# The ends of two mixers: norm weights and squares taken at the eviction, row sums accumulated in the residual sum

## Chip, core and metric

One core of one Trainium2 chip runs one program. The metric is device time in microseconds from start to end of an execution; the kernel before takes 2954.93 us, the median of three executions (2954.92 to 2955.82).

## What is computed

Two transformer-like blocks run one after the other over 1024 positions of width 1024, all in float32. Only the places where a mixer ends matter here.

```python
# first block, after its mixer (state space + Fourier + window attention)
y = concatenate([y_ssm, y_fft, y_att]) @ w_out
x = x + gt_m * rms_norm(y, g_post_mix)
h = rms_norm(x, g_pre_ffn) * (1.0 + sc_f) + sh_f
up = dwconv3(h @ w_up, conv_w, conv_b)
...
# second block, after its mixer (sparse attention + gated MLP)
m = mixer(x) ; x = layernorm(ALPHA * x + m, ln2_g, ln2_b)
x = layernorm(ALPHA * x + 0.5 * swiglu(x, ffn2_w1, ffn2_w3, ffn2_w2), ln3_g, ln3_b)
```

rms_norm divides by the root of the mean square of a row; layernorm takes off the mean of a row and divides by the root of its variance. Both then multiply by a weight per column, and layernorm adds a bias per column.

## The kernel before

The 1024 positions are eight row tiles (n = 0 to 7) of 128 positions; the width is eight column tiles (k = 0 to 7). Each product of float32 is three products of upper and lower parts (fp32r), so each operand is first split: ScalarE writes the upper part (a cast), VectorE the lower part (source less upper part). TensorE, VectorE, ScalarE and SyncE each have an order of instructions written out by hand, and semaphores between them (`wait_ge`, `then_inc`).

**The mixer's last product** (`down_tensor`, `down_products` L1083). It has two halves of four row tiles. Each half accumulates over eight steps and leaves the four rows in PSUM, two banks for a row (`y_banks(n)`). The first half is evicted while the second is multiplied, and its norm and residual sum are made there (`end_piece_scalar`, `end_piece_vector`). The change leaves that as it is. What it touches is what comes behind the second half, when the rows 4 to 7 finish in the order 6, 7, 4, 5 (`last_rows`).

**What comes behind it** (`end_tensor_up`). The next stage is the product with the up weights. TensorE first transposes rows 0 to 3 (the left half of the new operand, columns k = 0 to 7, L2540) into the banks that the evicted rows leave, then makes the first "classic" product with each column (L1983) as soon as its lower part is there (`x_lo_made`); after that rows 4 to 7 in the same way (the right half). It can start to transpose rows 4 to 7 when these are complete: in the first mixer when they are scaled (`row_scaled`, L2187), in the second when the final row operation is done (`row_ready`, L2285).

**First mixer's end** (`end_scalar`, `end_vector` with e = 0). ScalarE evicts rows 6 and 4 by copies (L2213), VectorE rows 7 and 5 (L2247). VectorE scales and shifts each transposed column into `split_tmp` (L2378), ScalarE casts it (L2356), VectorE makes the lower part (L2372). Between odd columns ScalarE squares a row of y and sums it (`square_row` L2120). Then follow, with nothing of the split left: factors (`norm_factors`: mean square L2069, root on ScalarE L2058, five small steps in `inverse_root` L3731 to L3739), for each row `add_branch` (two multiplications by factor and norm weight L2180, one addition L2183), its square on ScalarE, factors again, and `scale_rows` (L2187). The norm weight is in `row_a`.

**Second mixer's end** (the same functions with e = 3). VectorE adds the residual while it evicts (L2253), makes the lower parts straight from PSUM (L2372), and between columns 3 to 6 the moments of a row (`row_moments`, bn_stats L2191 and bn_aggr L2193). `last_factors` then centres and weights the rows (L2282), takes the roots and applies factor and bias (L2285).

**Behind both**: `upper_second` on ScalarE and `lower_second` on VectorE split the right half's columns, with four sums of parts ahead (`first_sum`, L1637). SyncE loads the weights (L1494) and stores the finished rows (`end_store` L2103).

Of the kernel before, what the change touches and what calls it, by code (L numbers as in the profile page):

```python
# [61 lines left out]
def body(ctx, nc, a, out):  # L62
# [764 lines left out]
    before = {"units": 0, "evac": 0, "ups": 0, "act": 0}  # L827

    class Down:


        def __init__(self, d, e, src, w, split_ahead, rest_ahead, first=None):
# [9 lines left out]
            before["evac"] += 4 if e < 2 else 2  # L842
# [148 lines left out]
    res_in, sq_done, var_ready, std_ready, row_ready = (sem(n) for n in ("res_in", "sq_done", "var_ready", "std_ready", "row_ready"))  # L991
    row_scaled, cols_turned, cols_hi, cols_ready = (sem(n) for n in ("row_scaled", "cols_turned", "cols_hi", "cols_ready"))
# [94 lines left out]
    def down_tensor(pe, st):  # L1087
        t = nc.tensor

        def step(half, k, kk, j, slot):  # L1090
# [3 lines left out]
            for n in rows_left:  # L1094
                if first and half:
                    pe.wait_ge((evac_act, evac_dve)[n % 2], st.evacs + n // 2 + 1)
# [1025 lines left out]
    def end_piece_scalar(act, st, i):  # L2122
        e = st.e
        if e == 0:
            if i == 0:
                act.wait_ge(evac_act, st.evacs + 2)
                act.wait_ge(evac_dve, st.evacs + 2)
# [21 lines left out]
    def end_piece_vector(dve, v, steps, st, i):  # L2149
# [12 lines left out]
        elif 0 <= i < 4:  # L2162
            dve.wait_ge(res_in, 16 * (NT * e + i + 1))
            if i == 0:
                dve.wait_ge(evac_act, st.evacs + 2)
                dve.wait_ge(evac_dve, st.evacs + 2)
# [37 lines left out]

    def end_scalar(act, st, up):

        s, e = nc.scalar, st.e
        for u in range(2):
            up_begin_scalar(act, up, u)
        if e == 0:  # L2210
            for n in (HN + 2, HN):
                st.wait_row(act, 1, n - HN)
                s.copy(y_row(n), y_banks(n)).then_inc(evac_act, 1)  # L2213
        upper_first(act, up)
        take_root(act, cols_of(1))
        if e == 0:
            for n in rows_of(1):
                square_row(act, n, True)
            take_root(act, cols_of(1))
        cast_op(act, up, 1, 0)  # L2220
        upper_second(act, up)

# [16 lines left out]

    def end_vector(dve, v, steps, st, up):  # L2240
# [3 lines left out]
        if e == 0:  # L2244
            for n in (HN + 3, HN + 1):
                st.wait_row(dve, 1, n - HN)
                v.tensor_copy(y_row(n), y_banks(n)).then_inc(evac_dve, 1)  # L2247
        else:
            dve.wait_ge(res_in, 16 * NT * (e + 1))
            for n in st.last_rows[1]:  # L2250
                n = HN + n
                st.wait_row(dve, 1, n - HN)
                v.scalar_tensor_tensor(res(n), y_banks(n), Y_SCALE[e], res(n), ALU.mult, ALU.add).then_inc(y_used, 1)  # L2253
        def moments_between(k):
            if 3 <= k < 3 + HN:
                row_moments(v, steps, HN + k - 3)

        if e:
            dve.wait_ge(y_used, HN)
        lower_first(dve, v, up, moments_between)  # L2260
        if e == 0:
            dve.wait_ge(evac_act, st.evacs + 4)
            dve.wait_ge(evac_dve, st.evacs + 4)
            dve.wait_ge(sq_done, 3 * HN)
            norm_factors(dve, v, steps, stat_a[:, cols_of(1)], cols_of(1))
            for n in rows_of(1):
                add_branch(dve, v, steps, n)
            dve.wait_ge(sq_done, 2 * NT)
            norm_factors(dve, v, steps, stat_c[:, cols_of(1)], cols_of(1))
            dve.wait_ge(xt_turned, up.turned(0, KD - 1))  # L2270
            scale_rows(v, 1)
        else:
            last_factors(dve, v, steps, e)
# [75 lines left out]
    def upper_first(act, up):  # L2349

        s, e = nc.scalar, up.e
        for k in range(KD):
            upper = x_columns(0, k)[0]
            if e == 0:
                act.wait_ge(xt_tmp, TMP_0 + k + 1)
                s.copy(upper, split_tmp[k % 2][:]).then_inc(x_hi_made, 1)  # L2356
            else:
                act.wait_ge(xt_turned, up.turned(0, k))
                s.copy(upper, turn_bank(k)).then_inc(x_hi_made, 1)
            if e == 0 and k % 2:  # L2360
                if k == 1:
                    act.wait_ge(evac_act, 4)
                    act.wait_ge(evac_dve, 4)
                square_row(act, HN + k // 2, False)

    def lower_first(dve, v, up, between=None):

        def rest(k):
            upper, lower = x_columns(0, k)
            dve.wait_ge(x_hi_made, up.turned(0, k))  # L2370
            src = split_tmp[k % 2][:] if up.e == 0 else turn_bank(k)
            v.tensor_tensor(lower, src, upper, ALU.subtract).then_inc(x_lo_made, 1)  # L2372
        if up.e == 0:
            for k in range(KD):
                dve.wait_ge(xt_turned, up.turned(0, k))
                if k >= 2:
                    dve.wait_ge(x_lo_made, up.turned(0, k - 2))
                v.tensor_scalar(split_tmp[k % 2][:], turn_bank(k), mod_cols[:, 3, k:k + 1], mod_cols[:, 2, k:k + 1],  # L2378
                                ALU.mult, ALU.add).then_inc(xt_tmp, 1)
                if k:  # L2380
                    rest(k - 1)
# [1925 lines left out]
```

## Time and profile before

| | |
|---|---|
| median of three executions | 2954.93 us |
| the profiled execution | 2953.73 us |
| its span | 2951.9 us |
| busy: TensorE, VectorE, ScalarE | 96%, 72%, 45% |
| mean granted TensorE clock | 0.981 of full |
| end of the first mixer | about 484 to 520 us |
| end of the second mixer | about 2271 to 2302 us |

The profile is one execution. TensorE's busy time overlaps with its loads of weights, so 96% means that it hardly ever has nothing under way, not that it runs at its peak. The full clock is 2.4 GHz; a granted clock of 0.5 is 1.2 GHz. All points in time are from the span's start.

### The profile page before, as it was taken

The page shows a single profiled execution, that of the slowest core. Times are in us where ns is not written, and L with a number is a line of the kernel's source. Part 1 is how long each engine was busy: PE and PEld are TensorE (multiplying, and loading weights), DVE is VectorE, ACT ScalarE, POOL GpSimd, SP SyncE. Part 2 cuts the span into 40 slices and gives each one's busy share as a digit, 9 for nine tenths or more (in the row PEclk, how much of TensorE's full clock was granted, in tenths as well). Part 3 has the DMA queues.
Part 4 walks back from the last instruction along what each step waited for, and adds up shares of the span by engine and source line. Part 5 has one row for each costly group of instructions (what it writes and reads, how often), then busy time and mean ns, then how long its engine had stood idle before and what let it go on. Part 6 is the DMA issues. An engine that isn't in the chain of part 4 may idle for free.

```text
span 2951.9 us, 37423 instructions
## 1 busy us (share of the span) xinstructions
PE 2820.3 (96%) x13573; PEld 2259.0 (77%) x13573; DVE 2119.2 (72%) x3861; ACT 1321.5 (45%) x2324; POOL 197.9 (7%) x250
## 2 busy tenths in 40 slices
PE   7998997999999999999999999999999899999997
PEld 4885676788888888788888887786677688888886
DVE  7888638888988567766666667798737866666568
ACT  3124745544444454433333453577743433333443
POOL 2050000000000000000000000223610000000000
PEclk9989999999999999999999999999999999999999
DMA  6542043244445884344447753211033344545864
GB/s 232 159 142 38 9 136 121 82 164 163 152 156 189 275 264 138 110 155 152 160 164 270 257 188 108 54 44 34 1 108 114 110 153 162 164 163 190 300 195 144
DMA packets 345413, 436.83 MB, mean 148 GB/s; under 512 B 29685, under 2 KB 191517, under 8 KB 345054
## 3 DMA queue, kind: packets, MB, share of 16 engines
q1 hardware_dynamic: 342274, 428.46, 44.5%
q10 hardware_dynamic: 2956, 5.99, 0.6%
q8 instruction: 108, 1.77, 0.2%
q14 instruction: 75, 0.61, 0.1%
HBM read 317.59 MB, written 116.50 MB: 147 GB/s over the span
## 4 chain that ended last, share of the span: by engine, by line
PE 79%; DVE 12%; ACT 4%; DMA 2%; issue 2%; POOL 1%; ACTq 0%; DVEq 0%; SPq 0%
PE psum L1992 37%; PE psum L1443 21%; PE psum L1083 5%; PE psum L2872 4%; PE psum L1983 3%; PE psum L4218 1%; DVE count_junk L3403 1%; PE psum L3075 1%; DMA ada_piece<-in_w_ada 1%; PE psum L3088 1%; PE psum L3062 1%; DMA x_rows<-in_x 1%; DVE x_t L1689 1%; ACT probs L499 1%; DVE ada_acc L3938 1%
## 5 line engine op out<-in xcount | busy, mean ns | idle before, releaser
L1443 PE MATMUL psum<-far_op,far_op 128*128 128x512 f32 x2772 | 629.6, 389 | 0.1
L1443 PEld LDWEIGHTS psum<-far_op,far_op 128*128 128x128 f32 x2772 | 520.2, 188 | 108.3 <-issue 0.5
L1992 PE MATMUL psum<-x_b,w_near 128*128 128x512 f32 x1440 | 346.0, 389 | 0.8 <-DVE w_near L1615 0.8
L1992 PE MATMUL psum<-x_t,w_near 128*128 128x512 f32 x1440 | 337.1, 389 | 2.3 <-ACT psum L1729 2.3
L1992 PE MATMUL psum<-x_t,w_far 128*128 128x512 f32 x1440 | 336.3, 389 | 0.0
L1992 PEld LDWEIGHTS psum<-x_t,w_near 128*128 128x128 f32 x1440 | 270.1, 188 | 59.5 <-ACT psum L1729 3.6
L1992 PEld LDWEIGHTS psum<-x_b,w_near 128*128 128x128 f32 x1440 | 270.3, 188 | 57.3 <-issue 1.2
L1992 PEld LDWEIGHTS psum<-x_t,w_far 128*128 128x128 f32 x1440 | 270.3, 188 | 56.4 <-ACT u_keep L1741 0.3
L1214 DVE TENSOR_TENSOR far_op<-far_a,far_op 128x512 fp32r<-128x512 f32 x231 | 159.7, 691 | 176.1 <-ACT far_op L1207 174.9
L1207 ACT CAST far_op<-far_a 128x512 fp32r<-128x512 f32 x231 | 143.9, 623 | 316.3 <-PE psum L1443 308.1
L1992 PE MATMUL psum<-x_b,w_far 128*128 128x512 f32 x720 | 177.9, 397 | 9.1 <-DVE val_row L1861 9.1
L1992 PEld LDWEIGHTS psum<-x_b,w_far 128*128 128x128 f32 x720 | 138.3, 193 | 39.4 <-DVE val_row L1861 10.3
L1615 DVE TENSOR_TENSOR w_far<-w_sum,w_far 128x512 fp32r<-128x512 f32 x120 | 82.3, 686 | 111.5 <-ACT w_far L1609 111.5
L1216 DVE TENSOR_TENSOR far_op<-far_b,far_op 128x512 fp32r<-128x512 f32 x231 | 159.1, 689 | 0.0
L3538 POOL TENSOR_TENSOR split_lo<-raw,split_hi 128x256 fp32r<-128x256 f32 (+1 forms) x60 | 44.8, 781 | 1642.2 <-ACT split_hi L2888 1642.2
L1208 ACT CAST far_op<-far_b 128x512 fp32r<-128x512 f32 x231 | 142.1, 615 | 0.0
L1615 DVE TENSOR_TENSOR w_near<-w_sum,w_near 128x512 fp32r<-128x512 f32 x120 | 80.9, 687 | 73.4 <-ACT w_near L1609 73.4
L1609 ACT CAST w_far<-w_sum 128x512 fp32r<-128x512 f32 x120 | 73.9, 616 | 114.3 <-PE psum L1992 114.3
L1609 ACT CAST w_near<-raw 128x512 fp32r<-128x512 f32 (+1 forms) x129 | 82.8, 642 | 70.5 <-PE psum L1992 59.1
L1615 DVE TENSOR_TENSOR w_far<-raw,w_far 128x512 fp32r<-128x512 f32 (+1 forms) x66 | 47.2, 715 | 84.8 <-ACT w_far L1609 84.8
L1060 DVE TENSOR_TENSOR src_lo<-yc_t,src_hi 128x512 fp32r<-128x512 f32 x31 | 21.4, 692 | 119.6 <-ACT w_out_hi L1053 119.5
L1983 PE MATMUL psum<-x_b,w_near 128*128 128x512 f32 x360 | 91.9, 406 | 7.3 <-DVE x_b L2372 6.4
(522 smaller groups left out, 4834.7 us busy)
## 6 DMA issues: line engine op xcount, KB each, us to landing
far_a<-row_ops SPq DMA_DIRECT2D x231, 256.0 KB, 2.9
row_ops<-hidden SPq DMA_DIRECT2D x99, 512.0 KB, 5.6
raw<-in_ffn_w SPq DMA_DIRECT2D x88, 512.0 KB, 4.3
col_sums<-hidden SPq DMA_DIRECT2D x66, 512.0 KB, 5.6
far_b<-col_sums SPq DMA_DIRECT2D x132, 256.0 KB, 3.5
raw<-in_w_up SPq DMA_DIRECT2D x44, 512.0 KB, 3.9
hidden<-in_ffn_w SPq DMA_DIRECT2D x44, 512.0 KB, 5.0
far_b<-in_ffn_w SPq DMA_DIRECT2D x66, 256.0 KB, 3.3
```

The costliest lines, as they stand in the source:

```text
L1083: ins = t.matmul(bank(2 * n + c), l[:, P * n:P * (n + 1)], r[:, HALF * c:HALF * (c + 1)], start=(first and m == 0), stop=(last and m == 2))
L1207: s.copy(far_a_hi[slot][:], far_a[late][t % FB][:]).then_inc(f_hi, 1)
L1208: s.copy(far_b_hi[slot][:], far_b[late][t % FB][:]).then_inc(f_hi, 1)
L1214: v.tensor_tensor(far_a_lo[slot][:], far_a[late][t % FB][:], far_a_hi[slot][:], ALU.subtract).then_inc(f_lo, 1)
L1216: v.tensor_tensor(far_b_lo[slot][:], far_b[late][t % FB][:], far_b_hi[slot][:], ALU.subtract).then_inc(f_lo, 1)
L1443: ins = t.matmul(bank(b + n), l[slot][:, rows], r[slot][:], start=(fresh and i == 0 and m == 0), stop=(i == FH - 1 and m == 2), skip_group ...
L1609: nc.scalar.copy(op_parts(p, i)[0], op_source(p, i)).then_inc(op_hi, 1)
L1615: nc.vector.tensor_tensor(lower, op_source(p, i), upper, ALU.subtract).then_inc(op_lo, 1)
L1983: ins = t.matmul(bank(b), at[:, l, cols], r, start=(first and m == 0), stop=(last and m == 2))
L1992: ins = t.matmul(bank(b), at[:, l, cols], x[:, k, r], start=(start and k == 0 and m == 0), stop=(k == 3 and m == 2), skip_group_check=not ...
L2872: ins = t.matmul(bank(2 * slot + half)[0:m], l[:, P * k:P * k + m], r[:, k, HALF * half:HALF * (half + 1)], start=(k == 0 and i == 0), sto ...
L3538: ins = g.tensor_tensor(tile_of(w_rest, m)[:, k:k + 2], tile_of(raw[slot], m)[:, k:k + 2], tile_of(w_top, m)[:, k:k + 2], ALU.subtract)
```

## The change

In the first mixer's end (`mix_end_scalar`, `mix_end_vector`) VectorE evicts all four rows and multiplies them by the norm weight as it does; ScalarE squares the rows straight from PSUM. A row's banks are read by one engine at a time, by turns. ScalarE scales, shifts and casts the left half's columns; VectorE makes the lower parts and, between them, the residual sum of a row with one instruction. The squares of the finished rows stand between the columns on ScalarE. Two rows are scaled on VectorE, two on ScalarE. One operand cast goes behind the second column of the right half.

In the second mixer's end the residual sum also accumulates the sum of its row. From it comes the negative mean; ScalarE squares the row with that as its bias and accumulates, between its casts; VectorE centres and weights a row behind it, between its lower parts. bn_stats and bn_aggr are gone there. The first half's waits on evictions now count each engine's by itself (`st.evacs`).

```diff
+    SQUARED, GAINED_FIRST = (2, 0, 3, 1), (2, 3, 1)
+    def mix_end_scalar(act, st, up):
+        def square_banks(n):
+            st.wait_row(act, 1, n)
+            act.wait_ge(sq_done, 2 * HN + SQUARED.index(n))
+            if n in GAINED_FIRST:
+                act.wait_ge(evac_dve, st.evacs[1] + 2 + left.index(n) + 1)
+            s.activation(sq_junk[:], y_banks(HN + n), ACT.Square, accum_out=stat_a[:, HN + n:HN + n + 1]).then_inc(sq_done, 1)
+        up_begin_scalar(act, up, 0)
+        up_begin_scalar(act, up, 1)
+        for n in SQUARED[:3]:
+            square_banks(n)
+        for k in range(KD):
+            act.wait_ge(xt_turned, up.turned(0, k))
+            if k >= 2:
+                act.wait_ge(x_lo_made, up.turned(0, k - 2))
+            s.activation(split_tmp[k % 2][:], turn_bank(k), ACT.Identity, scale=mod_cols[:, 3, k:k + 1],
+                         bias=mod_cols[:, 2, k:k + 1]).then_inc(xt_tmp, 1)
+            act.wait_ge(xt_tmp, TMP_0 + k + 1)
+            s.copy(x_columns(0, k)[0], split_tmp[k % 2][:]).then_inc(x_hi_made, 1)
+            if k == 0:
+                square_banks(SQUARED[3])
+                take_root(act, cols_of(1))
+            elif 3 <= k < 3 + HN:
+                square_row(act, HN + k - 3, True)
+                if k == 2 + HN:
+                    take_root(act, cols_of(1))
+        act.wait_ge(rstd_ready, 1)
+        act.wait_ge(xt_turned, up.turned(0, KD - 1))
+        for n in rows_of(1)[2:]:
+            s.mul(scaled_row(n), res(n), rstd(n)).then_inc(row_scaled, 1)
+        upper_second(act, up, lambda: cast_op(act, up, 1, 0))
+    def spread_rows(act, k):
+        at = {3: (0, 1), 4: (2,), 5: (3,)}.get(k, ())
+        if k == 3:
+            act.wait_ge(mean_ready, 1)
+        for i in at:
+            n = HN + i
+            if i:
+                act.wait_ge(spread_ready, i)
+            nc.scalar.activation(sq_junk[:], res(n), ACT.Square, bias=stat_c[:, n:n + 1],
+                                 accum_out=stat_a[:, n:n + 1]).then_inc(spread_ready, 1)
+        if k == KD - 1:
+            take_root(act, cols_of(1))
+    def mix_end_vector(dve, v, steps, st, up):
+        def gained(n):
+            st.wait_row(dve, 1, n)
+            if n not in GAINED_FIRST:
+                dve.wait_ge(sq_done, 2 * HN + SQUARED.index(n) + 1)
+            v.tensor_tensor(y_row(HN + n), y_banks(HN + n), wide(row_a), ALU.mult).then_inc(evac_dve, 1)
...
+        up_begin_vector(dve, up, 0)
+        for n in left[:2]:
+            gained(n)
+        up_begin_vector(dve, up, 1)
+        for n in left[2:]:
+            gained(n)
+        rest(0)
+        dve.wait_ge(sq_done, 3 * HN)
+        begin_factors(stat_a[:, cols_of(1)])
+        end_root(dve, v, steps, cols_of(1), False)
+        dve.wait_ge(evac_dve, st.evacs[1] + 2 + HN)
+        for k in range(1, 1 + HN):
+            rest(k)
+            n = HN + k - 1
+            dve.wait_ge(res_in, 16 * (n + 1))
+            v.scalar_tensor_tensor(res(n), y_row(n), rstd(n), res(n), ALU.mult, ALU.add).then_inc(row_ready, 1)
+        for k in range(1 + HN, KD - 1):
+            rest(k)
+        dve.wait_ge(sq_done, 2 * NT)
+        begin_factors(stat_c[:, cols_of(1)])
+        end_root(dve, v, steps, cols_of(1), False)
+        dve.sem_inc(rstd_ready, 1)
+        rest(KD - 1)
+        dve.wait_ge(xt_turned, up.turned(0, KD - 1))
+        for n in rows_of(1)[:2]:
+            v.tensor_scalar(scaled_row(n), res(n), rstd(n), None, ALU.mult).then_inc(row_scaled, 1)
+        lower_second(dve, v, up)
     def end_vector(dve, v, steps, st, up):
...
+            v.scalar_tensor_tensor(res(n), y_banks(n), Y_SCALE[e], res(n), ALU.mult, ALU.add,
+                                   accum_out=stat_c[:, NT + n:NT + n + 1]).then_inc(y_used, 1)
+        dve.wait_ge(y_used, HN)
+        steps.add(v.tensor_scalar(stat_c[:, cols_of(1)], stat_c[:, NT + HN:2 * NT], -1.0 / D, None, ALU.mult))
+        steps.settle()
+        dve.sem_inc(mean_ready, 1)
+        def centre_between(k):
             if 3 <= k < 3 + HN:
-                row_moments(v, steps, HN + k - 3)
+                n = HN + k - 3
+                dve.wait_ge(spread_ready, k - 2)
+                steps.add(v.scalar_tensor_tensor(res(n), res(n), stat_c[:, n:n + 1], wide(row_a), ALU.add, ALU.mult))
+            if k == 2 + HN:
+                steps.add(v.tensor_scalar(stat_a[:, NT + HN:2 * NT], stat_a[:, cols_of(1)], 1.0 / D, LN_EPS / ALPHA ** 2, ALU.mult, ALU.add))
+                steps.settle()
+                dve.sem_inc(var_ready, 1)
+        lower_first(dve, v, up, centre_between)
+        end_root(dve, v, steps, cols_of(1), False)
+        for n in rows_of(1):
+            v.scalar_tensor_tensor(res(n), res(n), rstd(n), wide(row_b), ALU.mult, ALU.add).then_inc(row_ready, 1)
...
     def end_tensor_up(pe, st, up):
             if e == 0:
-                pe.wait_ge((evac_act, evac_dve)[n % 2], st.evacs + (3 if n >= HN - 2 else 4))
+                at = st.last_rows[1].index(n)
+                pe.wait_ge(sq_done, 2 * HN + SQUARED.index(n) + 1)
+                pe.wait_ge(evac_dve, st.evacs[1] + 2 + at + 1)
```

`rest(k)` in `mix_end_vector` is the lower part of column k (L2372), and `begin_factors` the mean square (L2069).

## Rows read from the trace of the kernel before

**Rows 1.** The page's first part: busy us and share of each engine.
```profile
PE 2820.3 (96%) x13573; PEld 2259.0 (77%) x13573; DVE 2119.2 (72%) x3861; ACT 1321.5 (45%) x2324; POOL 197.9 (7%) x250
```
**Rows 2.** Waits of TensorE, 470 to 620: total us, times, longest.
```profile
PE psum L2540 <- DVE hidden L2187: 14.7, 1, 14.7
```
**Rows 3.** Waits of TensorE, 2260 to 2420.
```profile
PE psum L2540 <- DVE hidden L2285: 8.3, 1, 8.3
```
**Rows 4.** Windows, first mixer's end: busy by engine, granted clock, DMA share, GB/s.
```profile
488.00:501.00 13.00, 13.00 (x64) 10.48 (x64) 11.37 (x21) 7.74 (x15) 0.00 (x0) 1.00 0.09 23
501.00:515.70 14.70, 0.05 (x1) 0.00 (x0) 12.85 (x22) 5.74 (x10) 0.00 (x0) 0.63 0.38 143
515.70:519.80 4.10, 3.33 (x17) 3.09 (x17) 3.12 (x6) 2.85 (x5) 0.00 (x0) 0.65 0.00 0
...
545.00:580.00 35.00, 29.85 (x122) 23.37 (x121) 33.63 (x48) 17.10 (x28) 0.00 (x0) 0.95 0.35 113
```
**Rows 5.** Windows, second mixer's end.
```profile
2271.00:2277.00 6.00, 2.39 (x18) 1.71 (x16) 5.96 (x7) 2.14 (x4) 0.00 (x0) 1.00 1.04 321
...
2290.00:2298.40 8.40, 0.15 (x2) 0.02 (x1) 8.23 (x13) 0.00 (x0) 0.00 (x0) 0.71 0.30 111
2298.40:2302.00 3.60, 3.60 (x17) 3.60 (x18) 3.60 (x7) 1.80 (x4) 0.00 (x0) 0.50 1.03 354
```
**Rows 6.** In order of time, first mixer: start, us, instruction [idle before <-releaser].
```profile
482.14 1.92 ACT L2213 COPY hidden<-psum 128x1024 f32<-128x1024 f32 x2
...
483.49 2.35 DVE L2247 COPY hidden<-psum 128x1024 f32<-128x1024 f32 x2
...
487.98 1.66 PE L1983 MATMUL psum<-x_b,w_near 128*128 128x512 f32 x6 [2.00 <-DVE x_b L2372]
...
502.48 1.06 ACT L2120 ACTIVATE sq_junk<-hidden 128x1024 f32<-128x1024 f32 x1 [3.75 <-DVE hidden L2183]
503.45 0.19 ACT L2120 ACTIVATION_READ_ACCUMULATOR sq_junk<-hidden 128x1 f32 x1
...
512.92 2.74 DVE L2187 TENSOR_SCALAR hidden<-hidden,stat_b 128x1024 f32<-128x1024 f32 x4
515.57 2.49 DVE L1637 TENSOR_TENSOR b_sum<-x_b 128x512 f32<-128x512 f32 x4
...
515.72 3.32 PE L2540 MATMUL psum<-ident,hidden 128*128 128x128 f32 x16 [14.67 <-DVE hidden L2187]
...
518.91 0.78 ACT L2396 ACTIVATE xf_t<-psum,mod_cols 128x512 f32<-128x512 f32 x1
...
519.79 1.66 PE L1983 MATMUL psum<-x_b,w_near 128*128 128x512 f32 x6 [0.75 <-DVE x_b L2431]
```
**Rows 7.** In order of time, second mixer.
```profile
2271.67 4.61 DVE L2253 SCALAR_TENSOR_TENSOR hidden<-psum,hidden 128x1024 f32<-128x1024 f32 x4
...
2280.26 0.69 DVE L2372 TENSOR_TENSOR x_b<-psum,x_b 128x512 fp32r<-128x512 f32 x1
...
2281.03 0.59 ACT L2359 CAST x_b<-psum 128x512 fp32r<-128x512 f32 x1 [1.25 <-PE psum L2540]
...
2282.43 0.69 DVE L2372 TENSOR_TENSOR x_b<-psum,x_b 128x512 fp32r<-128x512 f32 x1
...
2287.67 4.87 DVE L2282 SCALAR_TENSOR_TENSOR hidden<-hidden,mean_var,row_a 128x1024 f32<-128x1024 f32 x4 [0.16 <-DVE stat_a L2074]
...
2293.46 4.87 DVE L2285 SCALAR_TENSOR_TENSOR hidden<-hidden,stat_b,row_b 128x1024 f32<-128x1024 f32 x4
...
2298.39 3.68 PE L2540 MATMUL psum<-ident,hidden 128*128 128x128 f32 x16 [8.25 <-DVE hidden L2285]
...
2301.71 2.54 PE L1983 MATMUL psum<-x_b,w_near 128*128 128x512 f32 x6
```
**Rows 8.** A line's instructions: ns min/median/max, first and last start, form.
```profile
L3683 ACT ACTIVATE x_rows<-x_rows,stat_b x4: 1132/1134/1148, 45.0 to 48.1; 128x1024 f32<-128x1024 f32 x4
```
**Rows 9.** Windows: a stretch of the first block's mixer.
```profile
264.00:270.00 6.00, 4.39 (x19) 1.83 (x20) 5.71 (x19) 2.04 (x8) 0.00 (x0) 0.66 0.01 3
```

More of the change, by code:

```diff
@@ L841, in __init__ @@
             before["units"] = self.end
-            before["evac"] += 4 if e < 2 else 2
+            before["evac"] = (2, 2 + HN)
         def operands(self, j, slot):
@@ L2205, in end_scalar @@
     def end_scalar(act, st, up):
-        s, e = nc.scalar, st.e
         for u in range(2):
             up_begin_scalar(act, up, u)
[L2210 to L2219, printed above, removed]
+        upper_first(act, up, lambda k: spread_rows(act, k))
@@ L2238, in far_end_scalar, with rest, begin_factors @@
             upper_columns(act, 1)
+    def mix_end_vector(dve, v, steps, st, up):
+        left = st.last_rows[1]
+        def gained(n):
[3 more added lines that the diff above has]
+            v.tensor_tensor(y_row(HN + n), y_banks(HN + n), wide(row_a), ALU.mult).then_inc(evac_dve, 1)
+        def rest(k):
+            upper, lower = x_columns(0, k)
+            dve.wait_ge(x_hi_made, up.turned(0, k))
+            v.tensor_tensor(lower, split_tmp[k % 2][:], upper, ALU.subtract).then_inc(x_lo_made, 1)
+        def begin_factors(sums):
+            steps.add(v.tensor_scalar(stat_a[:, NT + HN:NT + 2 * HN], sums, 1.0 / D, RMS_EPS, ALU.mult, ALU.add))
+            steps.settle()
[26 more added lines that the diff above has]
+            v.tensor_scalar(scaled_row(n), res(n), rstd(n), None, ALU.mult).then_inc(row_scaled, 1)
+        dve.wait_ge(x_lo_made, up.turned(0, KD - 1))
+        lower_second(dve, v, up)
     def end_vector(dve, v, steps, st, up):
@@ L2243, in end_vector @@
             up_begin_vector(dve, up, u)
[L2244 to L2253, printed above, removed]
@@ L2254, in moments_between @@
-        def moments_between(k):
-            if 3 <= k < 3 + HN:
-                row_moments(v, steps, HN + k - 3)
[L2258 to L2273, printed above, removed]
+        dve.wait_ge(res_in, 16 * NT * (e + 1))
@@ L2347, in kept_column, with upper_first, upper_second @@
         return t_part("t3", k % 4, k // 4)
-    def upper_first(act, up):
-        s, e = nc.scalar, up.e
+    def upper_first(act, up, between=None):
         for k in range(KD):
[L2353 to L2364, printed above, removed]
+            act.wait_ge(xt_turned, up.turned(0, k))
+            nc.scalar.copy(x_columns(0, k)[0], turn_bank(k)).then_inc(x_hi_made, 1)
+            if between:
+                between(k)
     def lower_first(dve, v, up, between=None):
-        def rest(k):
+        for k in range(KD):
             upper, lower = x_columns(0, k)
             dve.wait_ge(x_hi_made, up.turned(0, k))
[L2371 to L2381, printed above, removed]
-            rest(KD - 1)
-        else:
-            for k in range(KD):
-                rest(k)
-                if between:
-                    between(k)
-    def upper_second(act, up):
+            v.tensor_tensor(lower, turn_bank(k), upper, ALU.subtract).then_inc(x_lo_made, 1)
+            if between:
+                between(k)
+    def upper_second(act, up, between=None):
         s = nc.scalar
@@ L2415, in upper_second @@
                 upper(k)
+                if k == 1:
+                    between()
         else:
```

26 lines of the change are left out of this document (18 added, 8 removed).

## The prediction

> **What bounds the kernel now.** I read the page first, then who waited for whom on TensorE in the two stretches that the diff touches, then the busy times by window, then the instructions in order of time. TensorE is busy for 96% of the span [rows 1], so any time taken off a stretch in which it works without a break is not to be had; what can be had is TensorE's idle time. In the end of the first mixer it waits once for 14.7 us, for the row scaling of L2187 [rows 2], and in the end of the second once for 8.3 us, for the final row operation L2285 [rows 3]. These are TensorE's longest waits there by far. The windows show the second price of the two holes: the granted clock in and behind them is 0.63 and 0.65 of full in the first, 0.71 and 0.50 in the second, against 1.00 in the stretches ahead [rows 4, 5]. Sixteen transposes behind them take 3.32 and 3.68 us, and the first six products of the second mixer 2.54 us [rows 6, 7] where they take 1.66 us at the full clock (the row at 519.79).
>
> What fills the holes is VectorE and ScalarE working by turns. In the first mixer the split of the left half's columns ends at about 497; then come factors, for each of four rows two multiplications by half rows, an addition, and beside it the square on ScalarE; then factors again, four scalings, and only then the transposes at 515.72. ScalarE waits most of that time (3.75 us ahead of the first such square [rows 6]). In the second mixer VectorE alone is the chain from 2271.67 on: four residual additions, eight split operations with bn_stats and bn_aggr between them, four centrings, five root steps, four final operations, then the transposes at 2298.39; ScalarE waits (1.25 us ahead of each cast) [rows 7].
>
> **First mixer, part by part.** I rebuild the order of each engine from the diff, with today's durations.
>
> The start. ScalarE ends its second weight cast at 482.2 as before (a DMA sets that). VectorE has ended its first weight remainder at 480.7; the norm weights are now multiplied in at the eviction, four tensor_tensor from PSUM. The copies that they replace are 2.35 us for two, 1.2 each [rows 6], and I take 1.2 for the product too: rows 2 and 3 are out at 482.0 and 483.1, then the second weight remainder to 484.3, rows 0 and 1 at 485.8 and 486.9. The squares from PSUM are on ScalarE, 1.15 us each with the read of the accumulator (1.06 busy, the read overlapping; a square from SBUF [rows 6]): rows 2, 0, 3 end at 483.3, 484.5, 485.7. ScalarE then makes the first scaled and shifted column (0.78 us, a form it already runs in the second half [rows 6]), casts it, and VectorE has the remainder at 487.75. Today TensorE's first product of this stage is at 487.98, so nothing is lost at the start. Bounds of the PSUM square and product: from 1.0 us (the ScalarE copy from PSUM, 1.92 for two) to 1.3 (two-operand forms); over eight operations, most of them beside others, this is -0.3 to +0.7 us.
>
> The left half. ScalarE now carries, for each of eight columns, a scaled copy and a cast that waits for it: 0.78 + 0.07 + 0.53 = 1.38 us. The fourth square and a root stand behind column 0, and at columns 3 to 6 the square of a finished row, 1.13 more. VectorE makes the first factors at 488.2 to 489.7 (a root is 0.9 us of small steps: 2287.67 + 4.87 to 2293.46 [rows 7]), then for columns 1 to 4 a remainder (0.61) and one scalar_tensor_tensor that is the whole residual addition (1.22; form of rows 7). Step by step the columns are ready for TensorE at 487.8, 490.8, 492.7, 494.5, 496.3, 498.3, 500.7 and 503.65. TensorE needs 1.4 us for a column's six products (1.66 with the last one's tail) and 0.44 for four transposes behind each of the first four, so it follows at this pace with holes of at most 1.9 us and ends at 505.1; today it ends at 501.0 (0.05 us busy from then on [rows 4]) but then waits. The stage has moved from two phases to one, and ScalarE sets its pace.
>
> The end. The last square ends at 501.05, factors and root are at 502.6. VectorE does the last remainder (to 503.65) and scales two rows (to 505.0: four take 2.73 us today); ScalarE scales the other two at 1.13 each, a price that the same operation has elsewhere [rows 8], to 505.0. Transposes start at 505.1, today at 515.72: 10.6 us. Behind them the second half does today's work, with the operand cast L1609 now behind its second column; ScalarE waits for TensorE at most columns there, so that cast (some 1.0 us) is absorbed. If TensorE's clock has held, the first product follows 3.5 us after the transposes start (VectorE's four sums, 2.49 us, and a remainder) instead of 4.07 (515.72 to 519.79): 0.5 us more. In all 11.1 us. A chain of some 14 handovers between engines that I have put close together will slip; I take 0.05 us each, 0.7 us, and keep **10.4 us** (8.5 to 12).
>
> **Second mixer.** The residual addition from PSUM now also sums its row. No row here has such a VectorE form; the ScalarE one costs a read of 186 ns beside a main instruction of unchanged length [rows 6]. Below: no cost. Above: double the main instruction, 4 x 1.15 = 4.6 us. I take four reads of about 0.1 us net, 0.4 us: nearer to ScalarE's row, where the read mostly overlaps. The mean factor, one 128x4 operation and its signal, puts the first split remainder 0.3 us later, so the left half's products start 0.7 us later (2277.75) and end at 2290.8.
> The four bn_stats pairs with their bn_aggr go: today two remainders of 0.69 are 2.17 us apart (2280.26 to 2282.43), 1.55 of it for a row's moments. In their place, in the same slots, stand the centrings with the norm weight, 1.22 each, which today come behind (4.87 us); their squares are on ScalarE, 1.15 to 1.25 us each, in its idle time of 1.25 us between casts and the longer one ahead of the fifth [rows 7]. So the slot shrinks from 2.17 to 1.85 us and the 4.87 us behind it are gone. VectorE's chain: 2271.67 + 5.0 (additions) + 0.3 (mean) + 8 x 0.61 (remainders) + 4 x 1.22 (centrings) + 0.25 (variance) + 1.0 (root steps) + 4.87 (final) = 2292.85, and 0.2 for the last column's wait: transposes at 2293.05 against 2298.39, 5.3 us. TensorE's hole shrinks to 2.3 us. Today it is busy only 2.39 us between 2271 and 2277, with two holes of about 2 us, and the granted clock there stays 1.00 [rows 5], so I expect the full clock behind it: 1.7 us less for sixteen transposes and 0.8 for the first six products, of which VectorE's sums and remainder (2.49 + 0.69) hide a part. First product block ends at transposes + 4.35 instead of + 5.86 (2298.39 to 2304.25): 1.5 us. In all 6.8, less 0.2 of slips: **6.6 us**.
>
> The Trainium skill, "TensorE: Matmul & The Clock Gate", section "Part 1: The HAM clock gate", has the clock at 1.2 GHz after idleness and 2.4 GHz after sustained work; by it the recovered clock is a true gain here, and the two stretches at 0.65 and 0.50 agree. Against this change speaks "Vector Engine (DVE) Microarchitecture Reference", section "Points that are easy to get wrong", that a scalar_tensor_tensor with two fp32 SBUF sources has no port left for the accumulator and halves its throughput. Here one source is in PSUM, and the final operation L2285, with two SBUF sources, takes 1.28 us like the PSUM one, so no row bears it out; "VectorE: DVE Perf Modes", section "Two Vector instructions with no wait between them", says that an accumulator output is a second instruction, as it is on ScalarE in this trace.
>
> **Behind the two ends.** Each following stage is fed by weights that have landed long before (the pair after next is requested when the last is split), and all three engines move together, so I pass both gains on in full. The stores of rows start earlier with them, on a DMA share of 0.30 to 0.38 [rows 4, 5].
>
> Sum: 10.4 + 6.6 = 17.0 us. The profiled execution took 2953.73 us (span 2951.9 and 1.8 around it), so 2936.7; it lay 1.2 us under the median of the three runs, so the forecast for the median is **2937.9 us**.
>
> **Rivals.**
> *A. Summing costs as much as the addition itself.* Then the second mixer's additions take 4.6 us more, of which 0.4 is counted: 10.4 + 2.4 = 12.8 us, 2942.1. For it: no such row exists here. Against: ScalarE's accumulator leaves the main instruction unchanged. Chance 0.12.
> *B. Only one end gives its gain*, because the first mixer's left half, with ScalarE at 1.38 and 2.5 us a column, is a slower chain than I laid out (waits between scaled copy, cast, remainder and row that each hold the next), or because holes of up to 1.9 us now lie in all of it and the clock falls in the second half of the stage. Six microseconds lost: 11 us, 2944. For it: ScalarE has hardly any slack in my layout, and TensorE stood at 0.66 in a stretch where it was busy 4.39 of 6 us [rows 9]. Against: rows 5, where short holes left it at 1.00. Chance 0.12.
> *C. Slower.* The clock drops to its lower level at the first of the new holes in both ends and stays there through both second halves and the stage that follows. Each microsecond there at half clock costs half a microsecond of product time. To eat 17 us it needs 34 us at the lower level beyond what I have, and slower than before by 0.2% needs 46: (17 + 5.9) / 0.5. Some stretches do run low without long holes [rows 9]. Against: a dozen microseconds is all that either end shows today. It would give 2961 or more: chance 0.03.
> *D. The change is absorbed*: the stage behind is bound by VectorE or by a transfer that does not move, and under 6 us arrive, 2950. For it: VectorE is busy 33.6 of 35 us in 545:580, and TensorE waits for it there [rows 4]. Against: that work hangs on the same columns and moves with them. Chance 0.06.
>
> **Numbers.** The forecast has 0.67 (2934 to 2941), A 0.12, B 0.12, C 0.03, D 0.06. The range 2933 to 2944 holds the forecast's own, A and half of B, and at its lower end 2 us more than the layout gives, for slips that don't come and squares nearer to 1.0 us. A difference of 0.2%, 5.9 us, is what a measurement of this kernel can tell; faster by more: forecast, A, B and a little of D, 0.92; within it 0.05; slower 0.03.
>
> **What would show it.** In the profile after: TensorE's wait for the row scaling of the first mixer under 1 us instead of 14.7, and that for L2285's successor about 2.3 instead of 8.3; the granted clock at 1.00 behind both; from the first product of the left half to the first transpose of the right some 17.5 us (today 27.7) and 15.3 (today 21.3); the accumulating addition 1.2 us with a small second instruction; ScalarE busy above 0.85 in the first mixer's left half; no table load in either. Wrong would be: product gaps over 2 us between the columns, the first product of either stage over 1 us later after the last product of the mixer, or a new wait on DMA in the 50 us behind.

## The result

| | before | after |
|---|---|---|
| median (range), executions | 2955.38 us (2954.92 to 2957.04), 4 | 2938.60 us (2935.57 to 2939.63), 4 |
| the profiled execution: span | 2951.9 us | 2937.0 us |
| mean granted clock | 0.981 | 0.984 |

The ratio is 0.9936, 95% interval 0.9924 to 0.9948: faster by 0.64%, 18.9 us by the ratio. Forecast were 2937.9 us and a gain of 17.0 us.

**First mixer.** The waits of TensorE in the stretch 470 to 620 and then 2240 to 2400 (total us, times, longest):

```profile
PE psum L1984 <- DVE x_b L2296: 4.1, 5, 1.2
...
PE psum L1984 <- DVE x_b L2499: 1.5, 1, 1.5
...
PE psum L2610 <- ACT sq_junk L2218: 0.5, 1, 0.5
```
```profile
PE psum L1984 <- DVE x_b L2451: 2.2, 1, 2.2
PE psum L2610 <- DVE hidden L2362: 2.0, 1, 2.0
PE psum L2610 <- DVE hidden L2340: 1.8, 1, 1.8
```

The one wait of 14.7 us [rows 2] has become five of at most 1.2 us ahead of single columns, and the 8.3 us [rows 3] are 2.0. The 1.5 us stand ahead of the right half's first product (0.8 before), the 0.5 us ahead of a transpose that waits for a square. In order of time, the first end after:

```profile
485.49 1.02 ACT L2218 ACTIVATE sq_junk<-psum 128x1024 f32<-128x1024 f32 x1
...
487.49 1.03 PE L2610 MATMUL psum<-ident,hidden 128*128 128x128 f32 x8
...
494.05 1.28 DVE L2318 SCALAR_TENSOR_TENSOR hidden<-hidden,stat_b 128x1024 f32<-128x1024 f32 x1
...
501.50 1.66 PE L1984 MATMUL psum<-x_b,w_near 128*128 128x512 f32 x6 [0.18 <-DVE x_b L2296]
...
503.87 1.65 PE L1984 MATMUL psum<-x_b,w_near 128*128 128x512 f32 x6 [0.71 <-DVE x_b L2296]
...
505.87 2.19 ACT L2242 ACTIVATE hidden<-hidden,stat_b 128x1024 f32<-128x1024 f32 x2
...
506.74 1.66 PE L1984 MATMUL psum<-x_b,w_near 128*128 128x512 f32 x6 [1.21 <-DVE x_b L2296]
...
508.23 1.91 PE L2610 MATMUL psum<-ident,hidden 128*128 128x128 f32 x16
...
511.61 1.66 PE L1984 MATMUL psum<-x_b,w_near 128*128 128x512 f32 x6 [1.46 <-DVE x_b L2499]
```

The stretch ahead of this end is 3.42 us longer here (first transpose at 487.49, before at 484.07), so all points are compared by their distance from the first transpose of rows 0 to 3 (`ident` marks a transpose). The transposes of rows 4 to 7 start 20.74 us behind it (before 515.72 - 484.07 = 31.65 [rows 6]) and the right half's first product 24.12 (before 35.72): 11.6 us less. The sixteen transposes take 1.91 us, not 3.32 [rows 6]: the clock has held. By windows (busy of TensorE, its weight loads, VectorE, ScalarE, GpSimd; granted clock, DMA share, GB/s), first mixer and then second:

```profile
491.00:508.20 17.20, 14.00 (x64) 10.39 (x65) 12.94 (x27) 16.25 (x28) 0.00 (x0) 1.00 0.43 148
508.20:511.60 3.40, 1.94 (x17) 1.70 (x16) 2.96 (x6) 2.73 (x5) 0.00 (x0) 1.00 0.01 2
...
2282.10:2284.10 2.00, 0.04 (x1) 0.00 (x0) 2.00 (x3) 0.00 (x0) 0.00 (x0) 1.00 1.04 385
2284.10:2287.10 3.00, 2.98 (x16) 2.71 (x16) 3.00 (x6) 1.17 (x2) 0.00 (x0) 0.61 1.03 365
```

ScalarE is busy 16.25 of 17.2 us in the first end: it has become the fullest engine there. In the second end the granted clock is 0.61 behind the hole, against 0.50 [rows 5].

**Second mixer**, in order of time:

```profile
2263.30 1.22 DVE L2340 SCALAR_TENSOR_TENSOR hidden<-psum,hidden 128x1024 f32<-128x1024 f32 x1
2264.44 0.08 DVE L2340 DVE_READ_ACCUMULATOR hidden<-psum,hidden 128x1 f32 x1
2264.44 1.22 DVE L2340 SCALAR_TENSOR_TENSOR hidden<-psum,hidden 128x1024 f32<-128x1024 f32 x1
...
2267.99 0.17 DVE L2343 TENSOR_SCALAR stat_c<-stat_c 128x4 f32<-128x4 f32 x1
2268.25 1.15 ACT L2262 ACTIVATE sq_junk<-hidden,stat_c 128x1024 f32<-128x1024 f32 x1 [0.76 <-DVEq L2345]
...
2279.20 4.87 DVE L2362 SCALAR_TENSOR_TENSOR hidden<-hidden,stat_b,row_b 128x1024 f32<-128x1024 f32 x4
...
2284.12 3.11 PE L2610 MATMUL psum<-ident,hidden 128*128 128x128 f32 x16 [1.98 <-DVE hidden L2362]
...
2287.13 2.14 PE L1984 MATMUL psum<-x_b,w_near 128*128 128x512 f32 x6
```

From the first transpose (2264.67) it is 19.45 us to those of rows 4 to 7 (before 25.36 [rows 7]), and 35.86 to the first product with `w_far` (before 42.48): 6.6 us less. The four additions with their sums take 4.69 us from the first's start to the mean, before 4.64 to the first remainder: the sum costs 0.05 us for all four.

The account of the profiled spans: 11.6 + 6.6 won, 3.4 lost ahead of both ends, the rest equal within 0.2 us (first product of the first end's right half to the second end's first transpose: 1753.24 before, 1753.06 after). 18.2 - 3.4 = 14.8, and the spans differ by 14.9. That this middle stretch agrees so well is luck of the two traces: in the thirteen traces of this document it lies between 1749.1 and 1756.9 us.

### The profile page after: what moved, and what is told of

It reads as the page before. It is cut to its first block, busy times and chain, and to the rows that moved or that the text cites. A ratio compares the mean times of both kernels' runs of the same rounds, so it can differ in the third digit from the quotient of the medians.

```text
span 2937.0 us, 37417 instructions
## 1 busy us (share of the span) xinstructions
PE 2822.5 (96%) x13573; PEld 2257.0 (77%) x13573; DVE 2102.3 (72%) x3838; ACT 1331.9 (45%) x2340; POOL 197.2 (7%) x250
## 4 chain that ended last, share of the span: by engine, by line
PE 71%; DVE 8%; ACT 2%; POOL 1%; issue 1%; DMA 1%; DVEq 0%; SPq 0%; ACTq 0%
PE psum L1993 37%; PE psum L1444 21%; PE psum L2942 4%; PE psum L1984 3%; PE psum L1084 2%; DVE count_junk L3473 1%; PE psum L3145 1%; PE psum L3132 1%; PE psum L3158 1%; DVE x_t L1690 1%; DVE w_near L1616 0%; PE psum L3022 0%; ACT sign_junk L3239 0%; DMA raw<-in_ffn_w 0%; POOL p_wide L3640 0%
## 5 line engine op out<-in xcount | busy, mean ns | idle before, releaser
L1984 PE MATMUL psum<-x_b,w_near 128*128 128x512 f32 x360 | 90.8, 400 | 11.6 <-DVE x_b L2451 4.8
```

Source lines behind the costliest of these rows:

```text
L1984: ins = t.matmul(bank(b), at[:, l, cols], r, start=(first and m == 0), stop=(last and m == 2))
```

## Experiments

All distances in us from each end's first transpose of rows 0 to 3; "to rows 4-7" is their first transpose, "w_far" the first product with the far weights. They come from one trace of each kernel, and the last column is that one execution, which scatters by more than most of the differences between these kernels.

| kernel | first end: to rows 4-7 | to first product | second end: to rows 4-7 | to first product | to w_far | profiled time |
|---|---|---|---|---|---|---|
| before | 31.65 | 35.72 | 25.36 | 28.68 | 42.48 | 2953.73 |
| after | 20.74 | 24.12 | 19.45 | 22.46 | 35.86 | 2938.85 |
| first_only | 20.78 | 24.15 | 25.54 | 28.87 | 42.76 | 2942.38 |
| second_only | 33.16 | 37.23 | 19.45 | 22.46 | 37.71 | 2952.37 |
| weights_later | 24.04 | 27.41 | 19.46 | 22.46 | 35.73 | 2941.42 |
| vector_shapes | 24.15 | 27.53 | 19.46 | 22.46 | 35.92 | 2937.74 |
| few_squares | 18.39 | 21.77 | 19.45 | 22.46 | 37.73 | 2937.56 |
| moments_kept | 20.73 | 24.10 | 25.34 | 28.67 | 42.53 | 2946.40 |
| filled | 20.65 | 24.02 | 19.45 | 22.46 | 35.40 | 2933.92 |
| by_rows | 20.67 | 24.03 | 17.28 | 22.46 | 35.36 | 2932.55 |
| rows_sums | 20.71 | 24.07 | 17.31 | 21.18 | 34.08 | 2937.23 |
| best | 20.76 | 23.61 | 17.28 | 21.17 | 34.06 | 2941.78 |
| whole_again | 20.69 | 24.06 | 19.46 | 22.47 | 35.76 | 2936.90 |

### Each end alone

```diff
 first_only: end_scalar, end_vector as before
-        upper_first(act, up, lambda k: spread_rows(act, k))
+        upper_first(act, up)
+        take_root(act, cols_of(1))
 second_only: blocks_scalar, blocks_vector call the first end as before
```

> The first mixer's end is changed, the second is as before (bn_stats, centring behind the columns). Theory: each end gives its own gain and neither depends on the other. From TensorE's first transpose of rows 0 to 3 to that of rows 4 to 7 it takes 20.7 us in the first end, as with the whole change (31.65 before), and 25.4 in the second, as before; in time about 11.6 us less than before (ratio 0.9961). Rival (the gain in time is partly chance in the stretch ahead of the ends, or one end's gain depends on the other's): the distances come out as said but the time lies over 3 us away from 2943.8; or the second end's distance moves by over 0.5 us though nothing in it is changed.

> The second mixer's end is changed, the first is as before. Theory: the same distance is 31.65 us in the first end and 19.45 in the second (25.36 before), and the time 6.6 us less than before (ratio 0.9978). Rival (the ends depend on each other): the time is within 2 us of before, or the second end's distance is not 19.45 within 0.5.

Measured: first_only 2943.69 us, ratio 0.9953 (0.9940 to 0.9965); second_only 2952.37, ratio 0.9978 (0.9970 to 0.9987). 13.9 and 6.5 us (11.6 and 6.6 expected), together 20.4, against 18.9 with an interval of 3.5 to either side for the whole. Each gain is its own. One distance missed the expectation: second_only's unchanged first end took 33.16 us instead of 31.65. Its trace shows why: behind the hole of 1.93 us ahead of the first column the clock fell, and the second column's six products took 2.86 us, where the kernel before took 1.63 us behind the same hole (2.00 us [rows 6]):

```profile
488.79 1.72 PE L1984 MATMUL psum<-x_b,w_near 128*128 128x512 f32 x6 [1.93 <-DVE x_b L2430]
490.30 1.06 PE L2598 MATMUL psum<-ident,hidden 128*128 128x128 f32 x4
491.01 2.86 PE L1984 MATMUL psum<-x_b,w_near 128*128 128x512 f32 x6
```

> The whole change once more, beside before and best on one chip. Theory: the stretch from each end's first transpose to its right half is as in the first trace (20.74 and 19.45 us, 24.12 and 22.46 to the first product) within 0.1 us, while the stretch ahead of the first end lies anywhere between 484 and 488 us, by the granted clock between 150 and 300 us; ratio to before 0.9937 (0.992 to 0.995). Rival (the changed program costs 3.4 us ahead of the first end, since its first trace had the first transpose at 487.49 where before had 484.07): it is at 487 to 488 again and the ratio is 0.9949.

Measured: 2936.00 us (2932.67 to 2937.11), ratio 0.9927 (0.9914 to 0.9940); first transpose at 485.23 us; the distances in each end within 0.1 us. So at least most of the 3.4 us ahead of the first end was chance and not the price of the changed program: in the eleven traces with the new first end the first transpose lies between 484.26 and 488.57 us, in the two with the old one (before, second_only) at 484.07 and 484.95; a price of a microsecond is not excluded. The traces differ there in the granted clock too, 0.85 to 0.89 from 150 to 300 us in the five traces in which I read it.

### What sets the pace in the first end

```diff
 weights_later
-            v.tensor_tensor(y_row(HN + n), y_banks(HN + n), wide(row_a), ALU.mult).then_inc(evac_dve, 1)
+            v.tensor_copy(y_row(HN + n), y_banks(HN + n)).then_inc(evac_dve, 1)
...
-            v.scalar_tensor_tensor(res(n), y_row(n), rstd(n), res(n), ALU.mult, ALU.add).then_inc(row_ready, 1)
+            add_branch(dve, v, steps, n)
 vector_shapes
-            s.activation(split_tmp[k % 2][:], turn_bank(k), ACT.Identity, scale=..., bias=...).then_inc(xt_tmp, 1)
+            v.tensor_scalar(split_tmp[k % 2][:], turn_bank(k), ..., ALU.mult, ALU.add).then_inc(xt_tmp, 1)
...
 few_squares
-                square_row(act, HN + k - 3, True)
...
+                s.activation(sq_junk[:, :, 0:8], res(n)[:, :, 0:8], ACT.Square, accum_out=stat_c[:, n:n + 1]).then_inc(sq_done, 1)
```

few_squares leaves most of a row out of its sum, so its factors are not those of the computation: it is of use for its times alone.

> Whole change, but in the first end VectorE evicts by plain copies and applies factor, norm weight and residual sum with the two half-row multiplications and the addition of before (2.6 us a row instead of 1.2), between the same columns. Theory 1 (the work of VectorE and ScalarE in the left half is the pace, the moved place alone is not enough): 1.4 us more of VectorE at columns 1 to 4, of which ScalarE's own pace (2.4 us a column from the third on) hides 0.6 at two of them; the distance from the first transpose to that of rows 4 to 7 grows from 20.7 to 24 to 26 us. Theory 2 (what was won is the order, work beside products instead of behind them, and the fused multiplication is worth nothing here): it stays within 0.7 us of 20.7.

Measured: 24.04 us to rows 4-7, 3.3 more. The evictions take the same time in both (2.35 us for two copies, 2.34 for two products); what costs is the old form of the row, which leaves holes of 1.07 to 1.53 us ahead of columns 2 to 5. The fused form is worth that: work moved beside the products pays only as far as the engine has room between two columns. Theory 1 stands.

> Whole change, but in the first end VectorE scales and shifts the left half's columns (0.81 us each), as before, and ScalarE only casts and squares. Theory 1 (ScalarE sets the pace at columns 3 to 6, VectorE at 1 to 4, with the load nearly even): VectorE then has 2.6 us at each of columns 1 to 4, ScalarE 1.6, and the distance to the transposes of rows 4 to 7 grows by 1 to 3 us over 20.7. Theory 2 (ScalarE's chain is the only bound): it shrinks by 1 us or more.

Measured: 24.15 us, 3.4 more (1 to 3 expected), of which not all is VectorE's load. The first column comes 1.4 us later (5.03 us behind the first transpose instead of 3.61), the hole ahead of it is 2.27 us and the clock falls behind it:

```profile
489.29 2.93 PE L1984 MATMUL psum<-x_b,w_near 128*128 128x512 f32 x6 [2.27 <-DVE x_b L2291]
...
492.73 2.79 PE L1984 MATMUL psum<-x_b,w_near 128*128 128x512 f32 x6
```

Theory 2 falls: ScalarE is not the only bound. How much of the 3.4 us is the late start and how much the fuller columns, this run does not part.

> Whole change, but the four squares of the finished rows in the first end are taken over 16 of their 1024 elements only (left out: the rest of the sum). ScalarE's chain is 0.85 us shorter at each of columns 3 to 6. Theory 1 (ScalarE's chain holds the last three columns and the last root): the holes ahead of columns 5, 6 and 7 (0.18, 0.71, 1.21 us) go but for the last's root, and the distance shrinks from 20.7 to 18.2 to 19.2 us. Theory 2 (VectorE's rows and TensorE's products bind): under 0.5 us are won.

Measured: 18.39 us, 2.35 less, and TensorE waits for no column behind column 1:

```profile
499.27 6.40 PE L1984 MATMUL psum<-x_b,w_near 128*128 128x512 f32 x24
505.51 1.91 PE L2613 MATMUL psum<-ident,hidden 128*128 128x128 f32 x16
```

So ScalarE's squares hold the last three columns. Its second end, untouched, shows 37.73 us to w_far against 35.86: again the clock, with the first six products at 2.93 us.

### What won in the second end: less work for VectorE, or the place of the centring

```diff
+                row_moments(v, steps, n)
+                steps.add(v.scalar_tensor_tensor(res(n), res(n), mean_var[:, n, 0:1], wide(row_a), ALU.subtract, ALU.mult))
```

> Whole change in the first end; in the second bn_stats and bn_aggr stay on VectorE, without the row sums and without ScalarE's squares, but each row is centred and weighted between the columns, right behind its moments. Theory 1 (VectorE's work is the chain there, so only what leaves VectorE is won): the slot of a column is 0.61 + 1.55 + 1.22 = 3.4 us, TensorE waits for each of the columns 4 to 7, and the distance to the transposes of rows 4 to 7 is 25.0 to 25.6 us, as before the change (25.36). Theory 2 (what is won is that the centring stands between the columns): 20.5 us or less.

Measured: 25.34 us, as before the change (25.36). Two remainders are 3.36 us apart, and TensorE waits for two columns beyond the first, where four were expected (5.4 us in all, 1.9 of them ahead of the first column, where every version has a hole of about 2 us):

```profile
2274.01 0.68 DVE L2446 TENSOR_TENSOR x_b<-psum,x_b 128x512 fp32r<-128x512 f32 x1
...
2277.37 0.68 DVE L2446 TENSOR_TENSOR x_b<-psum,x_b 128x512 fp32r<-128x512 f32 x1
```

The place alone is worth nothing here, where VectorE is the chain; the gain is the variance that went to ScalarE.

### The hole of 2 us and the clock

```diff
 filled
+            if half and e == 3:
+                pe.wait_ge(x_lo_made, up.turned(0, 4))
+                for i in range(8):
+                    t.matmul(turn_bank(0), slot_of(3)[:, 1, 3 * P:4 * P], x_columns(0, KD - 1)[0], start=True, stop=True)
 by_rows (second end, right half, columns 0 to 3)
...
+                for n in range(HN):
+                    pe.wait_ge(row_ready, NT * e + HN + n + 1)
+                    for k in range(4):
+                        ins = t.transpose(turn_bank(k)[:, P * n:P * (n + 1)], res_block(HN + n, k), ident[:])
...
 rows_sums: by_rows, and in lower_second
-        for j in range(4):
+        for j in range(0 if late else 4):
             first_sum(dve, up, j)
...
+            if late and k >= 4:
+                first_sum(dve, up, k - 4)
...
 best: rows_sums, and in upper_second of the first mixer
             keep(0)
-            for k in range(KD):
+            upper(0)
+            keep(1)
+            for k in range(1, KD):
                 if k + 1 < KD:
                     keep(k + 1)
...
```

> Whole change; in the second end TensorE transposes rows 4 to 7 one after the other as each is finished, for the first four columns, instead of column by column when all four are there. It puts short work into the hole of 1.98 us behind which the clock was 0.61 of full. Theory 1 (the idle time lowers the clock): four transposes fall into the hole every 1.2 us, the last four follow the last row in 0.5 us, the granted clock behind it is above 0.9, and the first product of the right half comes 0.3 to 0.6 us earlier only, since VectorE's four sums (2.49 us) stand ahead of the first remainder; the six products behind it take 1.66 us. Theory 2 (the clock falls for another reason than idleness, for instance little work in the whole stretch): it is near 0.6 behind the last row as before and the first six products take 2.1 us or more.

> Whole change; in the second end TensorE makes eight more products of 512 columns into a bank that is free, without use, between the left half's last product and the transposes of rows 4 to 7, in column order as in the whole change. They take 1.75 us of the hole of 1.98. Theory 1 (the idle time ahead lowers the clock): the sixteen transposes take 1.9 us instead of 3.1, the six products behind them 1.7 instead of 2.1, and the first product of the right half comes 0 to 0.6 us earlier against the first transpose (22.46). Theory 2 (the clock falls there for another reason): 3.1 us and 2.1 as in the whole change. By rows the clock held in two of two traces, in column order it fell in two of two.

by_rows, then filled, then whole_again, TensorE in order of time:

```profile
2276.16 1.64 PE L2621 MATMUL psum<-ident,hidden 128*128 128x128 f32 x12
2278.34 0.66 PE L2621 MATMUL psum<-ident,hidden 128*128 128x128 f32 x4 [0.54 <-DVE hidden L2362]
2281.34 1.65 PE L1984 MATMUL psum<-x_b,w_near 128*128 128x512 f32 x6 [2.35 <-DVE x_b L2499]
```
```profile
2277.88 1.98 PE L2617 MATMUL psum<-x_b,w_near 128*128 128x512 f32 x8
2280.05 1.97 PE L2610 MATMUL psum<-ident,hidden 128*128 128x128 f32 x16 [0.20 <-DVE hidden L2362]
2283.06 1.69 PE L1984 MATMUL psum<-x_b,w_near 128*128 128x512 f32 x6 [1.04 <-DVE x_b L2499]
```
```profile
2282.58 3.27 PE L2610 MATMUL psum<-ident,hidden 128*128 128x128 f32 x16 [2.01 <-DVE hidden L2362]
2285.59 2.04 PE L1984 MATMUL psum<-x_b,w_near 128*128 128x512 f32 x6
```

In all six traces with the hole of about 2 us (after, whole_again, second_only, weights_later, vector_shapes, few_squares) the sixteen transposes take 2.45 to 3.27 us and the first six products 2.04 to 2.93. In the four traces in which TensorE has work there (filled, by_rows, rows_sums, best) the products take 1.65 to 1.69 us and w_far comes at 35.4 us or earlier instead of 35.7 to 37.7. Work in this place keeps the clock: theory 1, as far as this place goes. By rows the granted clock from the last row on is 1.00. The length of a single hole does not decide it, though: by_rows passes a hole of 2.35 us right behind, at the full clock, and in all thirteen traces TensorE passes the two holes at the start of the second end, of 1.8 and of 1.9 to 2.2 us, without loss: the first six products behind them take 1.65 to 1.69 us. What else decides is not shown. The first product itself does not move (22.46, where by_rows was expected to bring it 0.3 to 0.6 us forward), since VectorE's sums stand ahead of it.

> As by_rows, and VectorE's four sums of the left half's parts go from ahead of the right half's remainders to behind its columns 4 to 7 (second end only). Theory: the sums set the first product of the right half, so it comes at 1.4 us behind the last finished row instead of 3.1, and 1.7 us are won over the whole change, 2936 to 2937 us by ratio 0.9930 to before. Rival (ScalarE's casts and the transposes set it as much): under 0.6 us are won. Other rival: the sums, moved behind, delay the differences that the next stage waits for, and the gain is lost there as a wait of the x_t products.

Measured: 2934.09 us (2931.98 to 2940.42), ratio 0.9922 (0.9908 to 0.9935; 0.9930 expected). The first product comes 1.28 us earlier than in by_rows, 1.8 us behind the last finished row (expected 1.4: ScalarE's cast comes first, VectorE waits 1.04 us for it), and w_far 1.28 us earlier. The stretch behind has no new wait, but it does not keep its length: from w_far to the end of the span it takes 637.7 us, against 636.6 in by_rows. TensorE waits once there for VectorE in every kernel, 3.0 to 3.6 us long, and the twelve products behind that wait take 5.49 us instead of 4.50 (rows_sums, then by_rows):

```profile
2340.04 5.49 PE L1993 MATMUL psum<-x_b,w_far 128*128 128x512 f32 x12 [3.54 <-DVE val_row L1862]
```
```profile
2336.46 4.50 PE L1993 MATMUL psum<-x_b,w_far 128*128 128x512 f32 x12 [3.35 <-DVE val_row L1862]
```

best shows the same 5.49 us, and so do second_only and few_squares, in which the sums were not moved; from w_far to the end these four take 637.3 to 637.7 us, the other nine 636.1 to 636.6. So most of the 1.28 us was lost again in both traces that won it, and whether the moved sums are the cause is not shown.

> Whole change with rows transposed as they finish and the four sums behind the columns in the second end, and in the first end ScalarE's cast of the right half's first column ahead of its second scaled copy. Theory: 0.5 us at the first end (24.1 to 23.6 from the first transpose to the right half's first product), 1.3 to 1.8 at the second; against the whole change in the same runs about 2 us, 0.07%. Rival: the cast waits for its own scaled copy (0.07 us), so the rest of the columns are later by as much and nothing is won by the last one.

Measured: 2938.12 us (2930.52 to 2941.78), ratio 0.9936 (0.9924 to 0.9948), beside 2936.00 us and 0.9927 for the whole change in the same session. In the trace 0.45 us are won at the first end's right half, but all but 0.1 are lost again by the w_far product (36.84 against 36.97): the rival there was right. The second end's 1.7 us stand as far as w_far; 1.4 of them are lost again behind it (637.6 us to the end of the span, 636.2 in whole_again). The time does not show them: executions of one kernel differ by 4 to 11 us, and in best's trace the stretch between the two ends took 1756.9 us against 1753.8 in whole_again's, with a clock of 0.95 against 0.98 from 2050 to 2200. Neither best nor rows_sums is shown to beat the change in time.

## Why the prediction was right

**First end, step by step.** The prediction had the columns ready at 487.8, 490.8, 492.7, 494.5, 496.3, 498.3, 500.7 and 503.65 and the transposes at 505.1. Less the 3.42 us of the stretch ahead, the trace has 487.7, 490.8, 492.6, 494.4, 496.3, 498.1, 500.5, 503.3 and 504.8. Both the mechanism (ScalarE's chain of scaled copy, cast and square, VectorE beside it) and the sizes hold: the square from PSUM is 1.02 us, the products at the eviction 2.34 for two, the fused row 1.28, two scalings on ScalarE 2.19 (from [rows 8]). The 0.7 us set aside for slips did not come, so 10.4 should have been left at 11.1; measured 11.6.

**Second end.** The row sums were charged 0.4 us and cost 0.05, a read of 0.08 us that overlaps the next addition. The chain was 0.55 us shorter than laid out (19.45 against 20.0 to the transposes), so 5.9 us came there instead of 5.3, and the 0.2 us for slips were not needed. Against it, the step "I expect the full clock behind it" failed: a hole of 1.98 us was followed by 0.61, and transposes and first six products took 3.11 and 2.14 us instead of 1.9 and 1.66. The block of the first product ended 5.15 us behind the first transpose (3.01 + 2.14), where 4.35 were laid out and 5.86 taken before: 0.7 us won instead of 1.5. The clock is not all of it: in filled, where it held, the block still took 4.70 us (3.01 + 1.69), so the first product itself, behind VectorE's sums and remainder, was laid out 0.3 us too early. The errors cancel: 6.6 us forecast, 6.6 measured to w_far, and that is luck. The evidence used, that two holes of about 2 us between 2271 and 2277 left the clock at 1.00 [rows 5], was good for those two places, which all thirteen traces pass at the full clock, but not for another: behind the left half's products the clock fell in six traces of six. Even one place can go both ways, as the first hole of the old first end does in before and second_only.

**Passing on.** The stretches behind both ends kept their length within 0.2 us in the traces of before and after; with traces that scatter by 8 us between the ends this alone would show little, but the measured time, 18.9 us and at least 15.4 by its interval, leaves no room for rival D (under 6 us). Rival A falls by the read of 0.08 us. (The final row operation that the prediction holds against the doubled cost has no accumulator, so it is no test of it; an accumulating operation with both sources in SBUF was not run.) Rival B falls by the five waits of at most 1.2 us and by the gain of each end alone. C's drop does occur behind holes of 2 us, but for a few microseconds, not 34. Of the signs named, the short waits, the full ScalarE and the small second instruction came as said; the clock at 1.00 came only behind the first end.

**The sum.** 18.2 us by distances against 17.0 forecast; the time gave 18.9 with 15.4 to 22.5 in its interval. That the median fell within a microsecond of the forecast is partly luck: medians of the same two kernels in another session were 2957.11 and 2936.00, 21.6 us by their ratio.

## What to carry to other kernels

Work moved beside another engine's products pays as far as the slot between two of them has room: lay out the slot of each engine in microseconds, and fuse or hand over what doesn't fit. Where one engine was the chain, moving its work gained nothing (moments_kept) and taking work off it did. When executions scatter by more than the effect, compare distances inside the trace from a point just ahead of the change, and then look whether the stretch behind keeps its length: rows_sums won 1.28 us at one place and lost most of it behind a wait 42 us later.

## What the runs showed of the hardware

An accumulator read on VectorE behind a scalar_tensor_tensor with a PSUM source is a second instruction of 0.08 us, and the main one takes 1.22 us, against 1.21 without it; ScalarE's read takes 0.19 us. A hole of about 2 us in TensorE's work has no fixed price: in the traces here the clock stayed at 1.00 behind some (the two of before at 2273 and 2277, that of 2.35 us in by_rows) and fell towards its lower level behind others (0.61 behind the 1.98 us of the second end), and the idle place in the second end cost from 0.3 to 2.3 us against the kernel in which it was filled (35.73 and 37.73 against 35.40 to w_far).
